# First weight loads issued in step with what has landed, low-rank factors behind the third unit, and the sums of squares at the third unit's first product

## The chip, the cores and the metric

The kernel runs on one core of a Trainium2 chip. The time is that of one execution on the device in microseconds (us). The engines are TensorE (PE, with its weight loads as PEld), VectorE (DVE), ScalarE (ACT), GpSimd (POOL) and SyncE (SP), which issues the transfers (DMAs) concerned here.

## The reference

Two blocks follow each other, all in float32. The first takes 256 tokens and 16 meta tokens of width 2048, normalises them and multiplies them by `w_in` (2048 x 8320). The change lies in this stretch:

```python
hn = _rmsnorm(h_res, norm_in_g[l])        # x * rsqrt(mean(x*x) + eps) * g
P = hn @ w_in[l]
Pr, Pc = P[..., :RW_COLS], P[..., RW_COLS:]
prev = jnp.pad(Pr[:, :-1], ((0, 0), (1, 0), (0, 0)))
Pr = Pr + (prev - Pr) * mu_shift[l]       # r, k, v, g_r, wl (64 cols), al (64 cols)
w_raw = -softplus(-(w0[l] + tanh(wl) @ w_lora_up[l])) - 0.5
a = sigmoid(a0[l] + al @ a_lora_up[l])
```

A recurrence over the tokens, a gated convolution and an output projection follow, then the second block: two attention layers of width 4096 with their projections, and a last norm.

## The kernel before

The norm is taken out of the product: PE multiplies the weights by x times the gain, and the product is scaled afterwards by the inverse root of the mean square (`rms_inv`). Weights and x are each split into a high and a low part (ACT makes the high part, `split_hi`, line 254; DVE the low part, `split_lo`, line 260), and PE makes three matmuls for each 128 x 128 tile (`product`, lines 275 to 277).

Weights come in units of 2048 x 128, each loaded in two halves of 512 KB (8 tiles of k; a half is 24 matmuls). A unit's raw halves lie in one of three slots (`rawa`), the splits in four buffers. The first unit is the low-rank one (`U_LORA`), then for each tile i of 128 channels come `row_unit(i, 0)` to `row_unit(i, 3)` for k, r, v and g, and behind these the convolution's units. For i = 0 the second unit is thus `row_unit(0, 0)`, the third `row_unit(0, 1)`, the fourth `row_unit(0, 2)`. Products go to two PSUM banks in turn; a bank is free when its product has been taken (`taken`).

The order on each engine is written by hand, one function for each engine:

- SP (`first_sync`) issues the gain, chunks 0 and 1 of x (544 KB each) with the halves of the first unit between them, chunks 2 and 3, both halves of `row_unit(0, 0)`, the parameters `prm` (56 KB), `lmu` (0.5 KB), `lora` (512 KB, the low-rank factors), and then one unit after another. `load_columns` issues both halves of a unit; it waits only for the low parts of the unit that had the slot before, which the second and third unit have none of.
- ACT (`first_act`) makes the high part of x by chunks, and of the first unit between them; then the split of the second unit's first half, the squares of x (line 402) between the splits that follow, the copy of the first unit's product, the root (`setup_root`, line 416), and the tanh of the low-rank product (line 712). Splits run `AHEAD` = 3 halves ahead of the product. A split of a unit's first half waits until both halves of the unit have landed (`landed`), except in the very first unit.
- DVE (`first_dve`) makes the low parts, folds the four chunks of squares into one (`setup_fold`, line 412), takes the reciprocal of the root (line 435) and from there on scales, shifts and evacuates products (lines 811 to 833), makes the decay's scan (lines 860 to 865) and the bonus product (line 881).
- PE (`first_pe`) runs the units in order. Smaller products are slipped in between tiles by a table of functions: `setup_sums` (line 430, four matmuls with ones, which sum the squares over the partitions) before tile 4 of the second half of `row_unit(0, 0)`; `gates(0)` (line 607) before tile 6 of the second half of `row_unit(0, 1)`; then `key_norm` (615) and `bonus` (622).

In `product` the wait for the low part of the half stands ahead of the loop over the tiles, and the slipped-in function is called inside that loop.

Of the kernel before, what the change touches and what calls it, by code (L numbers as in the profile page):

```python
# [29 lines left out]
P = 128  # L30
# [4 lines left out]
L = SEQ + META  # L35
CH = 1024
# [114 lines left out]
def wait(eng, sem, value):  # L151

    if isinstance(value, int) and value <= 0:
        return
    eng.wait_ge(sem, value)
# [7 lines left out]
def _build(nc, A, top):  # L163
# [3 lines left out]
    def sem(name):  # L167
        return top.enter_context(nc.semaphore(name))
# [6 lines left out]
    hi_ready = sem("hi_ready")  # L175
# [171 lines left out]
    x_in = [sem(f"x_in{c}") for c in range(4)]  # L347
# [17 lines left out]
    xh, xl = xhl[:, :, 0:L], xhl[:, :, 272:272 + L]  # L365
# [6 lines left out]
    def setup_loads(sp, c):  # L372
        if c == 0:
            sp.dma_start(gain[:], A["gain"]).then_inc(gain_in, 16)
        sp.dma_start(x0[:, chunks[c]], A["xt"][:, chunks[c]]).then_inc(x_in[c], 16)
# [49 lines left out]
    def setup_sums(pe):  # L425
        pe.wait_ge(pool_seq, 7)
        pe.wait_ge(sq_folded, XC - 1)
        n = KT // XC
        for k in range(n):
            mm = nc.tensor.matmul(psum[2][:, 0:L], ones[:], sq0[:, k], start=k == 0, stop=k == n - 1)  # L430
        mm.then_inc(rms_bcast, 1)
# [39 lines left out]
    FIRST = [0, META - 2, 0, META - 2]  # L471
    FIRST_CONV = [META - 2] * 4

    def first_phase():
# [6 lines left out]
        st = Stream(ph, "a", 3, 0, sem("begin_in"))  # L481
# [48 lines left out]
        w_in = A["w_in"].rearrange("(k p) n -> p k n", p=P)  # L530
        R_KINDS, C_KINDS = [1, 0, 2, 3], [5, 6, 4, 7]

        def row_unit(i, n):
            return At(U_IN + 4 * i + n)

        def conv_unit(i, n):
            return At(U_IN + 4 * CT + 4 * i + n)
# [9 lines left out]
        def first_sync(sp):  # L547
            low_rank = slice(4 * CH, 4 * CH + P)
            setup_loads(sp, 0)
            st.load_half(sp, 0, 0, w_in[:, 0:8, low_rank], P, st.begin_in)  # L550
            setup_loads(sp, 1)
            st.load_half(sp, 0, 1, w_in[:, 8:16, low_rank], P, st.raw_in[0])
            for c in range(2, XC):
                setup_loads(sp, c)

            def keep_aab(i):

                sp.wait_ge(aab_taken, 2 * (i + 1))
                dst = aab_d.rearrange("(t c) (p e) s u -> c p e s t u", c=TC, e=2)
                for c in range(TC):  # L560
                    w = slice(C * c, C * c + C)
                    for e in range(2):
                        sp.dma_start(dst[c, i, e], aab[w, NT * e:NT * e + NT, w]).then_inc(aab_out, 16)
            for i in range(CT):
                for n in range(4):
                    if n == 1 and i >= 2:
                        keep_aab(i - 2)
                    st.load_columns(sp, row_unit(i, n), w_in,
                                    slice(R_KINDS[n] * CH + i * P, R_KINDS[n] * CH + (i + 1) * P))
                    if (i, n) == (0, 0):  # L570
                        sp.dma_start(prm[:], A["prm"]).then_inc(prm_in, 16)
                        sp.dma_start(lmu[:], A["lmu"]).then_inc(lmu_in, 16)
                        sp.dma_start(lora, A["lora"]).then_inc(lmu_in, 16)
            for i in range(CT):
                for n in range(4):
                    if (i, n) == (0, 1):
                        keep_aab(CT - 2)
                    if (i, n) == (1, 1):
                        keep_aab(CT - 1)
                    if (i, n) == (1, 3):  # L580
                        sp.wait_ge(sys_zeroed, 2)
                        sp.wait_ge(aab_out, 32 * TC * CT)
                        sp.dma_start(sa[:, 0:C], aab_d[0:NA].rearrange("c h s t -> (c h) s t")).then_inc(sys_in, 16)
                        sp.dma_start(sa[0:HEADS, last_block, 0:H2], aab_d[NA, :, 0:H2, 0:H2]).then_inc(sys_in, 16)
                    col = RW_COLS + (C_KINDS[n] - 4) * CH + i * P
                    st.load_columns(sp, conv_unit(i, n), w_in, slice(col, col + P))
            sp.wait_ge(sys_out[1], 1)
            sp.dma_start(inv_d[NA], sx_last).then_inc(stored, 16)
            sp.wait_ge(sys_out[0], 1)
            sp.dma_start(inv_d[0:NA].rearrange("c h s t -> (c h) s t"), sx[:, 0:C]).then_inc(stored, 16)  # L590
            sp.wait_ge(stored, 32)

        def first_pe(pe):
            x_chunk = {4 * j: (lambda n: lambda: pe.wait_ge(x_low, n))(j + 1) for j in range(2)}
            x_rest = {4 * j: (lambda n: lambda: pe.wait_ge(x_low, n))(j + 3) for j in range(2)}
            st.unit(pe, At(U_LORA), L, xh, xl, (x_chunk, x_rest))

            def gates(i):
                def emit():
                    if i == 0:  # L600
                        pe.wait_ge(lmu_in, 32)
                        pe.wait_ge(lora_ready, 2)
                        pe.wait_ge(pool_seq, 10)
                    wait(pe, z_used, 2 * i)
                    for e in range(2):
                        r = slice(64 * e, 64 * e + 64)
                        mm = nc.tensor.matmul(psum[2 + e][:, 0:L], lora[r, i * P:(i + 1) * P], low[r, :], start=True,
                                              stop=True)
                    mm.then_inc(z_ready, 1)
                return emit  # L610

            def key_norm(i):
                def emit():
                    pe.wait_ge(ksq_ready, i + 1)
                    nc.tensor.matmul(psum[4][:, 0:L], blk[:], t["ksq"][:, 0:L], start=True,
                                     stop=True).then_inc(n2_ready, 1)
                return emit

            def bonus(i):
                def emit():  # L620
                    pe.wait_ge(rkm_ready, i + 1)
                    nc.tensor.matmul(psum[5][:, 0:L], blk[:], t["tk"][:, 0:L], start=True,
                                     stop=True).then_inc(bonus_ready, 1)
                return emit

            def within(i):

                def emit():
                    pe.wait_ge(kap_made, i + 1)
                    wait(pe, aab_taken, 2 * i)  # L630
                    for n in range(NT):
                        w = slice(TT * n, TT * n + TT)
                        for e in range(2):
                            r = slice(64 * e, 64 * e + 64)
                            mm = nc.tensor.matmul(psum[6 + e][0:TT, w], bk[r, i, 0, w], kr[r, i, 0, w], start=True,
                                                  stop=True)
                            if n == NT - 1:
                                mm.then_inc(aab_sum, 1)
                return emit
            for i in range(CT):  # L640
                st.unit(pe, row_unit(i, 0), L, xh, xl, ({4: gates(i)}, {2: within(i - 1)}) if i else ({}, {4: lambda: setup_sums(pe)}),
                        FIRST[0])
                st.unit(pe, row_unit(i, 1), L, xh, xl, ({}, {}) if i else ({}, {6: gates(i)}), FIRST[1])
                st.unit(pe, row_unit(i, 2), L, xh, xl, ({2: key_norm(i)}, {}), FIRST[2])
                st.unit(pe, row_unit(i, 3), L, xh, xl, ({2: bonus(i)}, {}), FIRST[3])
            for i in range(CT):
                for n in range(4):
                    st.unit(pe, conv_unit(i, n), L, xh, xl, ({}, {2: within(CT - 1)} if (i, n) == (0, 0) else {}),
                            FIRST_CONV[n])
# [122 lines left out]
        def first_dve(dve):  # L772
# [170 lines left out]
            for i in range(CT):  # L943
                def p(n):
                    return prm[:, i, n:n + 1]
                for n in range(4):
# [22 lines left out]
                    if n == 3:  # L969
                        wait(dve, yb_made, i)  # L970
                        scaled(q, pgc[:], META, taken[q.bank()])
        ph.close()
        return first_sync, first_pool, first_pe, first_act, first_dve
    first_sync, first_pool, first_pe, first_act, first_dve = first_phase()
    p01.close()
# [528 lines left out]
    st = Stream(ph, "b", 4, U_WOUT)  # L1504
# [872 lines left out]
```

## Time and profile before

| | us |
|---|---|
| median of 3 runs | 2449.84 |
| lowest, highest | 2449.75, 2450.86 |
| profiled execution, time | 2450.07 |
| profiled execution, span | 2448.3 |

| engine | busy us | share of span |
|---|---|---|
| PE | 2419.5 | 99% |
| PEld | 2155.8 | 88% |
| DVE | 1753.6 | 72% |
| ACT | 1222.5 | 50% |
| POOL | 309.1 | 13% |

The span goes from the first to the last instruction of the profiled execution; its time has some 1.8 us around that. Busy time of an engine is what its instructions cover, register, branch, semaphore and DMA-issuing instructions left out. What counts for the time is the engine that others wait for, and where it is idle. The timeline prints, behind an instruction, how long its engine was idle before it and who released it.

### The profile page before, as it was taken

The page shows a single profiled execution, that of the slowest core. Times are in us where ns is not written, and L with a number is a line of the kernel's source. Part 1 is how long each engine was busy: PE and PEld are TensorE (multiplying, and loading weights), DVE is VectorE, ACT ScalarE, POOL GpSimd, SP SyncE. Part 2 cuts the span into 40 slices and gives each one's busy share as a digit, 9 for nine tenths or more (in the row PEclk, how much of TensorE's full clock was granted, in tenths as well). Part 3 has the DMA queues.
Part 4 walks back from the last instruction along what each step waited for, and adds up shares of the span by engine and source line. Part 5 has one row for each costly group of instructions (what it writes and reads, how often), then busy time and mean ns, then how long its engine had stood idle before and what let it go on. Part 6 is the DMA issues. An engine that isn't in the chain of part 4 may idle for free.

```text
span 2448.3 us, 40487 instructions
## 1 busy us (share of the span) xinstructions
PE 2419.5 (99%) x16586; PEld 2155.8 (88%) x16586; DVE 1753.6 (72%) x2629; ACT 1222.5 (50%) x1811; POOL 309.1 (13%) x397
## 2 busy tenths in 40 slices
PE   7999999999999999999999999999999999999998
PEld 7999999888888888888888888888888888888887
DVE  8998797997767566766766668667576757676676
ACT  6555433665544445444545456545444444444445
POOL 1212114422100000000000002111010001000011
PEclk9999999999999999999999999999999999999999
DMA  8666773486567666666666665777667766767783
GB/s 220 175 160 175 199 187 86 112 220 197 168 189 197 189 181 179 192 177 194 180 197 188 177 177 170 196 189 186 197 174 193 196 187 186 189 188 181 194 195 107
DMA packets 758344, 443.31 MB, mean 181 GB/s; under 512 B 28784, under 2 KB 721136, under 8 KB 758160
## 3 DMA queue, kind: packets, MB, share of 16 engines
q1 hardware_dynamic: 752880, 430.16, 63.3%
q0 software_dynamic: 5280, 10.56, 3.3%
q8 instruction: 132, 2.16, 0.4%
q14 instruction: 52, 0.43, 0.1%
HBM read 437.35 MB, written 3.31 MB: 180 GB/s over the span
## 4 chain that ended last, share of the span: by engine, by line
PE 81%; DVE 3%; issue 1%; ACT 0%; DVEq 0%; ACTq 0%
PE bank L295 40%; PE bank L299 20%; PE bank L325 5%; PE bank L326 5%; PE bank L329 5%; PE bank L1863 1%; PE bank L1882 1%; PE bank L1870 1%; PE bank L1862 1%; PE bank L1883 1%; DVE splitb L260 0%; PE bank L275 0%; PE bank L277 0%; PE bank L276 0%; PE bank L1843 0%
## 5 line engine op out<-in xcount | busy, mean ns | idle before, releaser
L295 PE MATMUL bank<-xx,splitb 128*128 128x512 f32 x3328 | 1166.1, 396 | 1.4 <-DVE mix L2152 0.8
L260 DVE TENSOR_TENSOR splitb<-rawb,splitb 128x1024 fp32r<-128x1024 f32 x672 | 834.7, 1255 | 395.0 <-ACT splitb L254 388.5
L254 ACT ACTIVATE splitb<-rawb 128x1024 fp32r<-128x1024 f32 x672 | 701.3, 1055 | 503.0 <-PE bank L299 354.1
L299 PE MATMUL bank<-xx,splitb 128*128 128x256 f32 x3328 | 922.4, 277 | 0.0
L295 PEld LDWEIGHTS bank<-xx,splitb 128*128 128x128 f32 x3328 | 625.3, 188 | 130.7 <-DVE mix L2152 1.1
L299 PEld LDWEIGHTS bank<-xx,splitb 128*128 128x128 f32 x3328 | 625.5, 188 | 1.6
L295 PE MATMUL bank<-oo,splitb 128*128 128x512 f32 x1008 | 343.3, 389 | 0.0
L275 PE MATMUL bank<-xhl,splita 128*128 128x258 f32 (+1 forms) x1040 | 297.7, 286 | 12.5 <-DVE splita L260 11.2
L277 PE MATMUL bank<-xhl,splita 128*128 128x258 f32 (+1 forms) x1040 | 292.6, 281 | 0.0
L276 PE MATMUL bank<-xhl,splita 128*128 128x258 f32 (+1 forms) x1040 | 292.3, 281 | 0.0
L299 PE MATMUL bank<-oo,splitb 128*128 128x256 f32 x1008 | 278.2, 276 | 0.0
L295 PEld LDWEIGHTS bank<-oo,splitb 128*128 128x128 f32 x1008 | 189.2, 188 | 39.6
L275 PEld LDWEIGHTS bank<-xhl,splita 128*128 128x128 f32 x1040 | 196.1, 189 | 17.7 <-DVE splita L260 11.6
L254 ACT ACTIVATE splita<-rawa 128x1024 fp32r<-128x1024 f32 x130 | 136.9, 1057 | 134.4 <-PE bank L277 131.9
L325 PE MATMUL bank<-splitb,xx 128*128 128x512 f32 x512 | 199.5, 390 | 0.0
L326 PE MATMUL bank<-splitb,xx 128*128 128x512 f32 x512 | 198.8, 388 | 0.0
L276 PEld LDWEIGHTS bank<-xhl,splita 128*128 128x128 f32 x1040 | 196.3, 189 | 0.7
L277 PEld LDWEIGHTS bank<-xhl,splita 128*128 128x128 f32 x1040 | 196.1, 189 | 0.0
L260 DVE TENSOR_TENSOR splita<-rawa,splita 128x1024 fp32r<-128x1024 f32 x130 | 164.9, 1275 | 34.6 <-ACT splita L254 33.4
L299 PEld LDWEIGHTS bank<-oo,splitb 128*128 128x128 f32 x1008 | 189.2, 188 | 0.0
L2011 ACT ACTIVATE cross<-bank 128x256 f32<-128x256 f32 x192 | 72.9, 380 | 205.7 <-PE bank L299 205.7
L329 PE MATMUL bank<-splitb,xx 128*128 128x512 f32 x512 | 126.4, 388 | 0.0
(294 smaller groups left out, 2265.6 us busy)
## 6 DMA issues: line engine op xcount, KB each, us to landing
rawb<-in_a_w_in_dram SPq DMA_DIRECT2D x256, 512.0 KB, 4.9
rawa<-in_w_in_dram SPq DMA_DIRECT2D x130, 512.0 KB, 5.4
rawb<-in_kv_w_dram SPq DMA_DIRECT2D x128, 512.0 KB, 4.8
rawb<-in_b_w_in_dram SPq DMA_DIRECT2D x128, 512.0 KB, 5.4
rawb<-in_a_w_out_dram SPq DMA_DIRECT2D x64, 512.0 KB, 5.3
rawb<-in_b_w_out_dram SPq DMA_DIRECT2D x64, 512.0 KB, 5.3
rawb<-in_w_out_dram SPq DMA_DIRECT2D x32, 512.0 KB, 5.1
table<-in_rel_dram POOLq DMA_DIRECT2D x32, 128.0 KB, 4.5
```

The lines of the kernel that those rows point to most:

```text
L254: nc.scalar.activation(self.parts(at, h)[0], self.raw_half(at, h), ACT.Copy).then_inc(hi_ready, 1)
L260: nc.vector.tensor_tensor(lo, self.raw_half(at, h), hi.bitcast(F32), ALU.subtract).then_inc(lo_ready, 1)
L275: nc.tensor.matmul(out, hi[:, w], rhs_hi(k), start=start and k == 0, stop=False)
L276: nc.tensor.matmul(out, hi[:, w], rhs_lo(k), start=False, stop=False)
L277: last = nc.tensor.matmul(out, lo[:, w], rhs_hi(k), start=False, stop=stop and k == 7)
L295: nc.tensor.matmul(out, hi[:, w], both(k).rearrange("p a t -> p (a t)"), start=start and k == 0, stop=False)
L299: last = nc.tensor.matmul(out[:, 0:SEQ], lo[:, w], both(k)[:, 0], start=False, stop=stop and k == 7)
L325: nc.tensor.matmul(out, xx[:, kt, 0, tokens], hi[:, w], start=kt == 0, stop=False)
L326: last = nc.tensor.matmul(out, xx[:, kt, 1, tokens], hi[:, w], start=False, stop=kt == KT - 1)
L329: last = nc.tensor.matmul(out, xx[:, kt, 0, tokens], lo[:, w], start=False, stop=False)
L1862: nc.tensor.matmul(SC[:, 0:P], qT[:, 0:P], kT[:, 0:P], start=True, stop=True)
L2011: a(cross[:, at.bank()], GB[at.bank()][:, SEQ:], ACT.Copy).then_inc(crossed, 1)
```

## The change

In SP's order, the first half of `row_unit(0, 0)` is issued when chunk 2 of x has landed, and the second half when chunk 3 has. The parameters and the first half of `row_unit(0, 1)` are issued when three halves of weights have had their high part made (`hi_ready` at 3: both halves of the first unit and the first of `row_unit(0, 0)`). The second half of `row_unit(0, 1)` is issued when `row_unit(0, 0)` has landed whole, then `lmu` and `lora`, which thereby stand behind `row_unit(0, 1)` instead of ahead of it. The fourth unit is issued when `row_unit(0, 1)` has landed whole. On PE, `setup_sums` moves from tile 4 of the second half of `row_unit(0, 0)` to tile 0 of the first half of `row_unit(0, 1)`, behind that half's wait for its low part. Nothing is computed otherwise.

```diff
--- before.py
+++ after.py
@@ -565,12 +565,23 @@
                 for n in range(4):
                     if n == 1 and i >= 2:
                         keep_aab(i - 2)
-                    st.load_columns(sp, row_unit(i, n), w_in,
-                                    slice(R_KINDS[n] * CH + i * P, R_KINDS[n] * CH + (i + 1) * P))
+                    cols = slice(R_KINDS[n] * CH + i * P, R_KINDS[n] * CH + (i + 1) * P)
                     if (i, n) == (0, 0):
+                        sp.wait_ge(x_in[2], 16)
+                        st.load_half(sp, 1, 0, w_in[:, 0:8, cols], P, st.raw_in[1])
+                        sp.wait_ge(x_in[3], 16)
+                        st.load_half(sp, 1, 1, w_in[:, 8:16, cols], P, st.raw_in[1])
+                    elif (i, n) == (0, 1):
+                        sp.wait_ge(hi_ready, 3)
                         sp.dma_start(prm[:], A["prm"]).then_inc(prm_in, 16)
+                        st.load_half(sp, 2, 0, w_in[:, 0:8, cols], P, st.raw_in[2])
+                        sp.wait_ge(st.raw_in[1], 32)
+                        st.load_half(sp, 2, 1, w_in[:, 8:16, cols], P, st.raw_in[2])
                         sp.dma_start(lmu[:], A["lmu"]).then_inc(lmu_in, 16)
                         sp.dma_start(lora, A["lora"]).then_inc(lmu_in, 16)
+                        sp.wait_ge(st.raw_in[2], 32)
+                    else:
+                        st.load_columns(sp, row_unit(i, n), w_in, cols)
             for i in range(CT):
                 for n in range(4):
                     if (i, n) == (0, 1):
@@ -638,9 +649,8 @@
                                 mm.then_inc(aab_sum, 1)
                 return emit
             for i in range(CT):
-                st.unit(pe, row_unit(i, 0), L, xh, xl, ({4: gates(i)}, {2: within(i - 1)}) if i else ({}, {4: lambda: setup_sums(pe)}),
-                        FIRST[0])
-                st.unit(pe, row_unit(i, 1), L, xh, xl, ({}, {}) if i else ({}, {6: gates(i)}), FIRST[1])
+                st.unit(pe, row_unit(i, 0), L, xh, xl, ({4: gates(i)}, {2: within(i - 1)}) if i else ({}, {}), FIRST[0])
+                st.unit(pe, row_unit(i, 1), L, xh, xl, ({}, {}) if i else ({0: lambda: setup_sums(pe)}, {6: gates(i)}), FIRST[1])
                 st.unit(pe, row_unit(i, 2), L, xh, xl, ({2: key_norm(i)}, {}), FIRST[2])
                 st.unit(pe, row_unit(i, 3), L, xh, xl, ({2: bonus(i)}, {}), FIRST[3])
             for i in range(CT):
```

## Rows read from the trace of the kernel before

**Rows 1.** The page's first part: engine, busy us, share of the span, instructions.

```profile
PE 2419.5 (99%) x16586; PEld 2155.8 (88%) x16586; DVE 1753.6 (72%) x2629; ACT 1222.5 (50%) x1811; POOL 309.1 (13%) x397
```

**Rows 2.** Windows: start:end, length, busy us (instructions) by engine, clock, DMA share, GB/s.

```profile
30.00:52.00 22.00, 21.25 (x165) 19.69 (x164) 20.06 (x32) 12.80 (x19) 5.22 (x5) 1.00 0.49 134
...
52.00:370.00 318.00, 318.00 (x2688) 311.94 (x2686) 278.33 (x419) 154.86 (x191) 62.12 (x64) 1.00 0.68 180
```

**Rows 3.** Timeline of PE: start us, us, engine, line, op, tiles, [idle before, releaser].

```profile
9.86 0.59 PE L275 MATMUL bank<-xhl,splita 128*128 128x272 f32 x1 [9.86 <-DVE splita L260]
...
19.45 0.39 PE L275 MATMUL bank<-xhl,splita 128*128 128x272 f32 x1 [1.37 <-DVE splita L260]
...
25.35 2.07 PE L430 MATMUL bank<-bk,ones 128*128 128x272 f32 x8 [0.93 <-DVE bk L412]
...
33.70 0.73 PE L607 MATMUL bank<-area 64*128 64x272 f32 x4
...
42.82 0.73 PE L622 MATMUL bank<-area,blk 128*128 128x272 f32 x2 [0.38 <-DVE area L881]
...
48.83 0.40 PE L275 MATMUL bank<-xhl,splita 128*128 128x272 f32 x1 [0.37 <-DVE area L811]
```

**Rows 4.** Timeline of ACT, columns as in rows 3.

```profile
17.08 1.06 ACT L254 ACTIVATE splita<-rawa 128x1024 fp32r<-128x1024 f32 x1 [1.67 <-DMA rawa<-in_w_in_dram]
...
23.00 1.05 ACT L254 ACTIVATE splita<-rawa 128x1024 fp32r<-128x1024 f32 x1
...
27.46 0.49 ACT L416 ACTIVATE rms_inv<-bank,eps 128x272 f32<-128x272 f32 x1 [2.19 <-PE bank L430]
...
28.91 1.28 ACT L712 ACT_TABLE_LOAD   x1
...
31.69 0.43 ACT L712 ACTIVATE area<-area 64x272 f32<-64x272 f32 x1 [1.50 <-DVE area L833]
...
34.59 0.52 ACT L717 ACTIVATE area<-area,prm_sb 128x272 f32<-128x272 f32 x1 [0.92 <-DVE area L824]
```

**Rows 5.** Timeline of DVE, columns as in rows 3.

```profile
18.18 1.22 DVE L260 TENSOR_TENSOR splita<-rawa,splita 128x1024 fp32r<-128x1024 f32 x1 [1.91 <-ACT splita L254]
...
22.52 2.68 DVE L412 TENSOR_TENSOR bk<-bk 128x1088 f32<-128x1088 f32 x2
...
27.98 1.85 DVE L435 RECIPROCAL rms_inv<-rms_inv 128x272 f32<-128x272 f32 x1 [0.43 <-ACT rms_inv L416]
...
39.68 1.23 DVE L260 TENSOR_TENSOR splita<-rawa,splita 128x1024 fp32r<-128x1024 f32 x1 [1.11 <-ACT splita L254]
```

**Rows 6.** DMA issues from 3.29, 5.92, 6.39, 6.87, 14.82 us: KB, us to landing.

```profile
kr<-in_xt_dram SPq DMA_DIRECT2D x1, 544.0 KB, 8.7
...
kr<-in_xt_dram SPq DMA_DIRECT2D x1, 544.0 KB, 7.5
...
rawa<-in_w_in_dram SPq DMA_DIRECT2D x1, 512.0 KB, 8.8
...
rawa<-in_w_in_dram SPq DMA_DIRECT2D x1, 512.0 KB, 10.2
...
rawa<-in_w_in_dram SPq DMA_DIRECT2D x1, 512.0 KB, 7.3
```

**Rows 7.** DMA issues into an empty queue, from 35.66, 36.07, 43.93, 44.34 us.

```profile
rawa<-in_w_in_dram SPq DMA_DIRECT2D x1, 512.0 KB, 4.1
...
rawa<-in_w_in_dram SPq DMA_DIRECT2D x1, 512.0 KB, 5.4
...
rawa<-in_w_in_dram SPq DMA_DIRECT2D x1, 512.0 KB, 4.3
...
rawa<-in_w_in_dram SPq DMA_DIRECT2D x1, 512.0 KB, 6.1
```

**Rows 8.** Line groups of PE, 9.8 to 14 us, then 14 to 18 us.

```profile
L276 PE MATMUL bank<-xhl,splita 128*128 128x272 f32 x6 | 2.5, 411 | 0.0
...
L276 PE MATMUL bank<-xhl,splita 128*128 128x272 f32 x10 | 2.9, 285 | 0.0
```


## Prediction

> **What bounds the kernel now.** Units of weights are called u0 (low rank), u1, u2, u3 in the order of their loads, their halves a and b; the chunks of x are x0 to x3. I read the page's engine line first: TensorE (PE) is busy 2419.5 us of 2448.3 [rows 1]. Then the table of stretches: from 52 to 370 us PE has no idle time, and in the first 52 us it has what a change of the first loads can reach [rows 2]. Third, PE's timeline. It shows an idle start of 9.86 us; 1.37 us before unit 1's first half; 0.93 us before the sums of squares; 0.38 and 0.37 us at 42.82 and 48.83 us [rows 3]. Behind the start that is 3.05 us in all, and the start itself is set by u0 and the first two chunks of x, whose issue is untouched. So removing every later stall gives 3.05 us, 0.12%.
>
> ScalarE's (ACT's) timeline says which wait ends last: the split of u1 begins at 17.08 us, released by its DMA. It needs both halves of u1, though only half a is split there. u2's split at 23.00 us follows ACT's own work without idle time [rows 4]. The VectorE (DVE) timeline then gives the second chain: folds of the squares to 25.2 us, root, reciprocal from 27.98 us, and from there DVE and ACT hand to each other up to 39.68 and beyond [rows 5]. PE's waits at 42.82 and 48.83 us are for DVE, at the end of this chain [rows 3]. **The root of the mean square is therefore on the path that sets the end**, with no slack left at 42.82 us.
>
> Last, the DMA issues. The queue delivered in order and without a hole: x2 is landed at 3.29 + 8.7 = 11.99 us, x3 at 5.92 + 7.5 = 13.42, u1b at 6.87 + 10.2 = 17.07, u2b at 14.82 + 7.3 = 22.12 [rows 6]. Into an empty queue a half of 512 KB takes 4.1 to 4.3 us; the second of the pair lands 36.07 + 5.4 - 35.66 = 5.81 us or 44.34 + 6.1 - 43.93 = 6.51 us after the first one's issue [rows 7].
>
> **Part 1, waits ahead of u1's halves.** Half a is issued at 12.05 us instead of 6.39, half b at 13.5 instead of 6.87. Nothing else of SP's is due before them. Half a lands after 4.1 to 4.3 us, at 16.2 to 16.4; half b no earlier than 13.5 + 4.1 = 17.6, and by the pairs 1.7 us behind half a (39.76 to 41.47), so 17.9; by the slower pair 2.2 us behind (48.23 to 50.44), 18.6. I take 17.9, as half b's own latency points lower. ACT's split of u1a moves from 17.08 to 17.95 us: **+0.9**. Do x2 and x3 land sooner for it? They stood ahead of u1 in a queue that delivers in order; nothing to gain that I can see. PE begins u1 at 20.3 instead of 19.45 us.
>
> **Part 2, u2 behind the third split.** SP now waits until u1a is split: ACT start to DVE start was 17.08 to 18.18, 1.10 us [rows 4, 5], so 19.05 us. Queued behind this wait are prm, u2 and u3, lmu and lora. prm costs 0.4 us of issue and 56 KB. u2a is issued at 19.5 us, u2b at 19.9 instead of 14.82 (its wait on u1 is long over). u2b lands 5.8 to 6.5 us after 19.5: 25.3 to 26.0 instead of 22.12. Two rows lie at either end, so I take the middle, 25.65.
> ACT is ready for u2a at 23.00 + 0.9 = 23.9 us, so it now waits some 1.7 us for data. Split 25.65, plus 1.10 to DVE, plus 1.27 to PE (18.18 to 19.45 [rows 3, 5]): u2a's low part is ready at 28.0 us.
>
> **Part 3, the sums of squares behind the wait of u2's product.** DVE's folds end near 25.2 + 0.9 = 26.1 us. PE, from 20.3 us: it did one and a half halves in 25.35 - 0.93 - 19.45 = 4.97 us [rows 3], at most 3.3 per half, so u1 is done by 26.9. Left in place, the sums would start at 26.1; at the new place they start when the low part of u2a is ready, 28.0. They take 25.35 to 27.46 = 2.11 us to the root [rows 3, 4]: root at 30.1 instead of 27.46, **+2.65**. The 0.93 us stall is gone, and about 1.1 to 1.5 us before the sums stand in its place.
>
> **Part 4, lora and lmu behind u2.** Issued at 20.4 to 20.8 us, queued behind u2b: 27 us. DVE needs lmu only behind the reciprocal (27.98 + 1.85, plus 2.65: 32.5 us), PE needs lora later. Cover of over 5 us, cost nothing; uncovered, it would cost what exceeds that.
>
> **Part 5, u3 behind the landing of u2.** Issue 25.7 us, landed both halves 31.5 to 32.2 [rows 7]; 2.7 us after u2b u3a would have queued anyway, so this wait is felt less. ACT can then split u3a (1.07 us), load its table (1.28 us): ready at 33.9 to 34.6. The tanh was at 31.69 [rows 4] and moves with the root to 34.3. So +0 to 0.3 there, and PE's gate products (33.70 [rows 3]) come to 35.2 or so: PE waits a little. None of this sets the end, because ACT's square of k (34.59 [rows 4]), on DVE's chain, moves to 37.2 and the tanh of the gates follows it. u4 and u5 are issued behind u3 and lie over 4 us ahead of their splits.
>
> **Sum.** The chain root, reciprocal, low-rank shift, k, scan, exponentials, split of u4, PE's waits at 42.82 and 48.83 us contains no DMA that is now late and no PE step that ends last, so it moves as a whole: PE is 2.65 us later at 45.5 us. Behind it PE is never idle up to 370 us [rows 2], and the other engines move with it. The profiled execution took 2450.07 us (span 2448.3), 0.23 above the median of the three; 2450.07 + 2.65 - 0.23 = **2452.5 us**. That is +0.11%, within the 0.2% (4.9 us) that a measurement of this kernel can tell from no change.
>
> The bounds of this case: if half b of u1 lands at 17.6 and u2 after 5.8, the shift is 2.65 - 0.3 - 0.35 = 2.0; at 18.6 and 6.5, 2.65 + 0.7 + 0.35 = 3.7: 2451.8 to 2453.5.
>
> **A rule that speaks otherwise.** The rows give 4.1 to 4.3 us for a lone half. The Trainium skill (DMA: Bandwidth & Descriptors, section Anatomy of one DMA) gives a fixed 2.0 us plus bytes at 436 GB/s, measured on GpSimd's path: an estimate of 3.2 us here, 4.4 for the pair. By it the reloads would nearly catch up, which is rival A's outcome; the rows here, on SP's queue, are longer.
>
> **Rivals.**
> A. **The loads stay hidden.** If the waits shorten each load's own time (fewer packets in flight), by 1.4 us on the last half of each pair, u1 lands as before and u2b by 23.8 us. Then u2a is ready at 23.8 + 2.4 = 26.2, PE finishes u1 at 25.6 to 26.1, and the root is at 28.3: +0.2 to +0.9 us, 2450.0 to 2450.8. For it: u1b took 10.2 us from its issue [rows 6], so the queue was full. Against: the rows from an empty queue already hold that advantage.
> B. **The change gains.** If the reloads are hidden and the 0.93 us stall counted on PE's path, PE ends 0.5 to 1 us earlier: 2449. Against: PE then waits at 42.82 us, since DVE's chain does not move forward.
> C. **The clock falls, ending on the slower side.** PE's idle time ahead of u1 grows from 1.37 to 2.2 us, a length that no stretch between PE's first matmul and the end shows. Matmuls of the same shape took 411 ns at PE's start and 285 ns once it had worked for about 4 us [rows 8]: the two levels, 1.2 and 2.4 GHz, although the printed granted clock doesn't resolve it. If the level falls there, u1a's 24 matmuls cost 24 x 0.126 = 3.0 us; 1.1 to 1.3 are covered by the wait for u2, the rest delays the root: 2454.2 to 2454.5.
> D. **Round trips add up.** Three load pairs in series (u1, u2, u3), each at the 6.5 us end, and lora's 512 KB between u2 and u3: u1b 18.6, u2b 26.8, u3b 33.4 to 34.7 us. The latter decides from 32.3 us on, as ACT's split and table load then hold the tanh: +4 to +5 us, 2454 to 2455; with C, over +4.9, slower by more than 0.2%.
> E. **The waits do nothing** (all met on arrival): 2449.8 to 2450.1. Against: x2 and x3 land 5.6 and 6.6 us after u1's present issues (11.99 - 6.39, 13.42 - 6.87) [rows 6].
>
> **Chances.** Forecast 0.62; A with E 0.14; B 0.05; C 0.07; D 0.12, of it 0.03 beyond 4.9 us. Range from A's lower end to D's beginning, 2450.0 to 2454.3, leaves out B, a part of C and D. Faster by over 0.2%: 0.01, since only 3.05 us are to be had. Slower by over 0.2%: 0.03. Within: 0.96.
>
> **What would show it.** Landing of u1b at 17.6 to 18.6 and u2b at 25 to 26.5 us; ACT idle about 1.7 us, released by DMA, before the split of u2a; the sums right before u2's first product at about 28 us; the root at 30; PE idle over 1 us at about 45 us for DVE L881; then PE without a gap to 370 us. The prediction is wrong if x3 or u1 lands earlier than now, if u2's split doesn't wait for data, or if the root moves by 2.65 us and the end doesn't.

## The result: slower by 3.7 us, and where it arises

The changed kernel took 2453.75 us (median of 20 runs, 2451.54 to 2455.7) against 2450.01 us for the kernel before (20 runs, 2448.31 to 2451.61). The ratio is 1.0015, with a 95% interval of 1.0009 to 1.0021: 2.2 to 5.1 us slower. The forecast was 2452.5 us, in a range of 2450.0 to 2454.3.

| | before | after |
|---|---|---|
| median, us | 2450.01 | 2453.75 |
| profiled execution, time | 2450.07 | 2454.09 |
| its span | 2448.3 | 2452.4 |
| PE busy, us | 2419.5 | 2420.1 |
| last chunk of x landed | 13.4 | 13.2 |
| u1a split begins (ACT) | 17.08 | 18.50 |
| u2a split begins (ACT) | 23.00 | 26.11 |
| sums of squares begin (PE) | 25.35 | 28.52 |
| root (ACT) | 27.46 | 30.63 |
| last early wait of PE ends | 48.83 | 52.00 |

The units are named as in the prediction (u0 to u3, halves a and b). ACT's timeline of the changed kernel answers to [rows 4]; the columns are start us, us, engine, line, operation, tiles, and the idle time before with its releaser:

```profile
18.50 1.06 ACT L254 ACTIVATE splita<-rawa 128x1024 fp32r<-128x1024 f32 x1 [3.11 <-DMA rawa<-in_w_in_dram]
...
26.11 1.06 ACT L254 ACTIVATE splita<-rawa 128x1024 fp32r<-128x1024 f32 x1 [1.59 <-DMA rawa<-in_w_in_dram]
...
30.63 0.49 ACT L416 ACTIVATE rms_inv<-bank,eps 128x272 f32<-128x272 f32 x1 [2.24 <-PE bank L430]
32.01 1.06 ACT L254 ACTIVATE splita<-rawa 128x1024 fp32r<-128x1024 f32 x1 [0.89 <-DMA rawa<-in_w_in_dram]
33.09 1.28 ACT L722 ACT_TABLE_LOAD   x1
34.87 0.43 ACT L722 ACTIVATE area<-area 64x272 f32<-64x272 f32 x1 [0.49 <-DVE area L843]
...
37.76 0.52 ACT L727 ACTIVATE area<-area,prm_sb 128x272 f32<-128x272 f32 x1 [0.93 <-DVE area L834]
```

Where ACT had one wait for weights before, of 1.67 us, it now has three: 3.11 us for u1, 1.59 for u2, 0.89 for u3. The root is at 30.63 instead of 27.46 us, 3.17 later, and so is everything behind it: the square of k (L727) at 37.76 instead of 34.59. PE's timeline answers to [rows 3]:

```profile
20.87 0.39 PE L275 MATMUL bank<-xhl,splita 128*128 128x272 f32 x1 [2.79 <-DVE splita L260]
...
28.52 1.84 PE L430 MATMUL bank<-bk,ones 128*128 128x272 f32 x7 [1.22 <-issue]
...
45.99 0.72 PE L633 MATMUL bank<-area,blk 128*128 128x272 f32 x2 [0.54 <-DVE area L891]
...
52.00 0.40 PE L275 MATMUL bank<-xhl,splita 128*128 128x272 f32 x1 [0.38 <-DVE area L821]
...
389.57 0.39 PE L275 MATMUL bank<-xhl,splita 128*128 128x258 f32 x1 [0.87 <-DVE cv L978]
...
2443.61 0.88 PE L1954 MATMUL bank<-sc,ones 128*128 128x128 f32 x4 [0.65 <-DVE sc L2329]
```

PE's stall before u1 has grown from 1.37 to 2.79 us, that before the sums from 0.93 to 1.22, and the wait for DVE's bonus product ends at 45.99 instead of 42.82 us. From 52.00 on PE is 3.17 us late, and it is 3.17 us late at 389.57 (386.40 before) too. At 2443.61 it is 4.01 us late. The 0.84 us between can't be put down to the change, because executions scatter by more than that behind the start: two executions of one kernel (e6 and e12 below) pass their last early wait at 46.87 and 46.82 us, 1.96 and 2.01 ahead of before, and this last PE row at 2436.57 and 2438.65, 3.03 and 0.95 ahead of before's 2439.60.

The windows of the start answer to [rows 2]; busy us (instructions) of PE, PEld, DVE, ACT and POOL, then clock, share of the DMA engines and GB/s:

```profile
10.00:20.00 10.00, 7.75 (x48) 7.29 (x48) 6.31 (x14) 6.60 (x13) 0.00 (x0) 1.00 0.58 186
20.00:30.00 10.00, 7.91 (x55) 7.31 (x56) 8.19 (x8) 6.80 (x8) 0.00 (x0) 1.00 0.84 239
...
55.00:373.00 318.00, 318.00 (x2687) 311.93 (x2687) 278.35 (x419) 154.87 (x191) 62.02 (x63) 1.00 0.68 180
```

Before, the same columns read, from 10 to 20 us:

```profile
10.00:20.00 10.00, 8.63 (x52) 8.26 (x53) 7.20 (x14) 8.04 (x14) 0.00 (x0) 1.00 1.13 328
```

The DMA engines moved 328 GB/s then and 186 now: the waits leave the queue empty from 18.5 us, where u1b has landed, to 19.6, and nearly so from 12 to 14 us (88 GB/s, before 309). The transfers themselves (issues from 11.97, 13.27 and 19.96 us; KB and us to landing) answer to [rows 6] and [rows 7]:

```profile
rawa<-in_w_in_dram SPq DMA_DIRECT2D x1, 512.0 KB, 4.1
...
rawa<-in_w_in_dram SPq DMA_DIRECT2D x1, 512.0 KB, 5.2
...
rawa<-in_w_in_dram SPq DMA_DIRECT2D x1, 512.0 KB, 4.4
```

u1a landed 4.1 us after its issue, u1b 5.2 us, so at 18.5 us; u2a 4.4 us, and ACT was released by u2b at 26.1.

### The profile page after: what moved, and what is told of

The parts are those of the page before. It is cut to its first block, busy times and chain, and to the rows that moved or that the text cites. A ratio compares the mean times of both kernels' runs of the same rounds, so it can differ in the third digit from the quotient of the medians.

```text
span 2452.4 us, 40488 instructions
## 1 busy us (share of the span) xinstructions
PE 2420.1 (99%) x16586; PEld 2155.5 (88%) x16586; DVE 1756.0 (72%) x2629; ACT 1222.7 (50%) x1811; POOL 307.7 (13%) x397
## 4 chain that ended last, share of the span: by engine, by line
PE 82%; DVE 2%; issue 1%; ACT 0%; DVEq 0%; ACTq 0%
PE bank L295 40%; PE bank L299 20%; PE bank L325 5%; PE bank L326 5%; PE bank L329 5%; PE bank L1873 1%; PE bank L1892 1%; PE bank L1880 1%; PE bank L1872 1%; PE bank L1893 1%; DVE splitb L260 0%; PE bank L275 0%; PE bank L277 0%; PE bank L276 0%; PE bank L1286 0%
```

## How the experiments are read

The loss is some 3 us of 2450, and the medians of 11 runs carry an interval of about +-2 us; e5, e7, e8, e9 and e10 have one execution each, whose time decides nothing. Positions in a trace are finer, but there is one trace for each kernel, and the landing of x shifts the whole start by up to 0.5 us between executions. So two distances are used. **D1** is when ACT begins to split u1a; it moves with the loads. **D2** is the time from there to the end of PE's last early wait. In the kernel before they are 17.08 and 48.83 - 17.08 = 31.75 us; in the changed kernel 18.50 and 33.50: +1.42 and +1.75, together 3.17. In the kernel with only `lora` moved D2 is 31.76, with D1 at 16.61, so D2 doesn't depend on the phase of x. D1 and the last mark do. The last column takes the phase out: it counts the last mark from where ACT begins on x2 (12.00 us in the kernel before, 11.97 in the changed one, 11.53 to 12.02 in all), so from 36.83 us in the kernel before.

| kernel | D1 | D2 | last mark | against 48.83 | the same, from x2 |
|---|---|---|---|---|---|
| before | 17.08 | 31.75 | 48.83 |  |  |
| after | 18.50 | 33.50 | 52.00 | +3.17 | +3.20 |
| e1, sums moved alone | 16.68 | 32.84 | 49.52 | +0.69 | +1.11 |
| e2, loads alone | 18.23 | 32.08 | 50.31 | +1.48 | +1.72 |
| e3, after, u1 at once | 16.80 | 33.93 | 50.73 | +1.90 | +1.97 |
| e4, after, u2 and u3 at once | 18.11 | 33.37 | 51.48 | +2.65 | +3.12 |
| e5, before, lora behind u2 | 16.61 | 31.76 | 48.37 | -0.46 | -0.04 |
| e6, before, u1a waited for alone | 15.14 | 31.73 | 46.87 | -1.96 | -1.78 |
| e7, before, one square first | 16.69 | 30.88 | 47.57 | -1.26 | -0.86 |
| e8, e2 without u3's wait | 18.45 | 31.78 | 50.23 | +1.40 | +1.47 |
| e9, e4 with PE kept busy | 18.78 | 32.84 | 51.62 | +2.79 | +3.20 |
| e10, after, u1a waited for alone | 16.09 | 33.39 | 49.48 | +0.65 | +0.63 |
| e11, e6 with squares on POOL | 15.13 | 34.61 | 49.74 | +0.91 | +1.09 |
| e12, e6 again | 15.08 | 31.74 | 46.82 | -2.01 | -1.77 |

The theory is that of the prediction: the root of the mean square heads a chain that PE waits for at 42.82 and 48.83 us, and three edits push it. The rival is that one part makes all of the loss, the others being hidden.

## The sums alone, and the loads alone

In e1 only the place of the sums differs from before, in e2 only the loads. The edit of e1, abridged to the tables of slipped-in functions that `row_unit(i, 0)` and `row_unit(i, 1)` get for i = 0:

```diff
-  row_unit(i, 0) ... ({}, {4: lambda: setup_sums(pe)})
-  row_unit(i, 1) ... ({}, {6: gates(i)})
+  row_unit(i, 0) ... ({}, {})
+  row_unit(i, 1) ... ({0: lambda: setup_sums(pe)}, {6: gates(i)})
```

> The kernel before, with only the sums of squares moved to the first product of u2. My theory (the root of the mean square is on the path, and the sums now stand behind u2a's low part): that part is made at 25.12 to 26.34 us, so the sums start at 26.4 instead of 25.35 us, the root at 28.5 instead of 27.46, and every later mark of PE (42.82, 48.83 us) comes 1.0 to 1.1 us later; PE stalls some 0.4 to 0.7 us ahead of the sums instead of 0.93. Time +1 us. Rival (the place of the sums is free, all of the loss is the loads'): root within 0.2 us of 27.46 and marks unmoved.

Measured: D2 +1.09 us. The sums began at 26.04 us, 9.36 us behind u1a's split, where before it was 8.27:

```profile
26.04 1.84 PE L430 MATMUL bank<-bk,ones 128*128 128x272 f32 x7 [0.54 <-issue]
```

DVE makes u2a's low part only behind its folds, so the sums now wait for one instruction more, which ended at 25.93:

```profile
24.71 1.22 DVE L260 TENSOR_TENSOR splita<-rawa,splita 128x1024 fp32r<-128x1024 f32 x1
```

The stall before the sums shrank from 0.93 to 0.54 us, and yet the root came later: a shorter stall of PE at this place is not a gain, as PE does u1's last four tiles first and has the root wait for it and for u2a. The median was 2451.67 us, ratio 1.0005 (0.9996 to 1.0014), which alone decides nothing. The marks do: the rival, a free place, is out.

> The changed order of the loads alone; the sums stay inside the second half of u1. My theory: u1's split at 18.5 us shifts the folds by 1.4 us, the sums start at 26.7, the root is at 28.9, marks +1.4 us; u2's later landing (26.1 us) costs nothing, as PE is busy with the sums and the rest of u1 until 30.2 us. So of the 3.17 us of the changed kernel the two parts give 1.05 + 1.4 alone, and 0.7 us arises only where both are together. Rival (the late u2 costs by itself): marks +2 us or more, with PE idle before u2's first product.

Measured: D1 +1.15 (+1.39 counted from x2), D2 +0.33, the last mark +1.48; ratio 1.0006 (0.9997 to 1.0015). The root was at 28.60 us, +1.14, all of it D1. The expectation missed that the mark came 0.34 us later than the root. ACT's timeline shows what took over:

```profile
28.60 0.49 ACT L416 ACTIVATE rms_inv<-bank,eps 128x272 f32<-128x272 f32 x1 [0.45 <-PE bank L430]
31.84 1.07 ACT L254 ACTIVATE splita<-rawa 128x1024 fp32r<-128x1024 f32 x1 [2.75 <-DMA rawa<-in_w_in_dram]
32.93 1.28 ACT L723 ACT_TABLE_LOAD   x1
34.22 0.43 ACT L723 ACTIVATE area<-area 64x272 f32<-64x272 f32 x1
```

The root was made in time, but then ACT waited 2.75 us for u3, and the table load for the tanh stands behind u3a's split. The tanh starts at 34.22 us with no idle time before it, 5.62 us behind the root; before, it was 31.69 - 27.46 = 4.23, and released by DVE [rows 4].

To see whether that is u3's wait, e8 takes the wait out of e2.

```diff
-                        sp.wait_ge(st.raw_in[2], 32)
```

> The kernel of the run with the loads alone (sums at their old place), without the wait for u2's landing ahead of u3. There the root was at 28.60 us (+1.14) but PE's last early wait at 50.31 (+1.48); u3 landed at 31.8, ACT split its half a at 31.84 and loaded the table of the tanh behind it. Theory (u3's landing takes over by 0.34 us): u3 lands near 29.5, and the last mark comes as much later than 48.83 us as the root than 27.46, so +1.1 to +1.2. Rival (the 0.34 us come from the gate products or from PE's order): root and mark stay apart by 0.3 us or more.

Measured: D2 31.78 us, before's own, with root and mark at +1.36 and +1.40. So ACT's split of u3a, released by the DMA at 30.94 instead of 31.84 us, was in time; the 0.33 us were u3's wait. The root came 0.2 us later than expected, with D1 (18.45). In the changed kernel the same wait costs nothing: u3a is split at 32.01, and the tanh at 34.87 is released by DVE after 0.49 us of idle time.

## Each wait taken out of the changed kernel

```diff
# e3
-                        sp.wait_ge(x_in[2], 16)
...
-                        sp.wait_ge(x_in[3], 16)
# e4
-                        sp.wait_ge(hi_ready, 3)
...
-                        sp.wait_ge(st.raw_in[1], 32)
...
-                        sp.wait_ge(st.raw_in[2], 32)
```

> The changed kernel without the two waits ahead of u1's halves; all else as changed. My theory: u1 lands at 17.1 us again, u1a is split by 18.2, and from there u2b takes the 6.5 us that it took in the changed kernel: 24.7 us, the sums start at 27.1, the root at 29.2, marks +1.7 to +1.8 us instead of +3.17. Rival (u2's wait alone sets the root, u1's throttling is hidden, for example because x2 and x3 land sooner with it): marks stay at +3.2 us, x3 lands later than 13.24 us.

Measured: D1 back at 16.80, D2 33.93, the last mark at +1.90; ratio 1.0009 (1.0 to 1.0018). The rival falls: u1's waits are not hidden. D2 is 0.43 us longer than in the changed kernel, as ACT was released by u2b 8.02 us behind u1a's split there (24.82 - 16.80) and 7.61 in the changed kernel (26.11 - 18.50). x3 landed at 13.3 us there and at 13.2 in the changed kernel, so holding u1 back brought x 0.1 us at most.

> The changed kernel without the three waits around u2 and u3, those ahead of u1's halves kept. My theory: u1 as in the changed kernel (split at 18.5 us), u2b lands at about 22.1, well before ACT comes to it at 24.4 us; its low part is ready at 27.8, root at 29.9, marks +2.4 to +2.5 us. Rival (the loss comes from u2's wait alone): marks back to +1.05 us or less.

Measured: +2.65 us at the last mark (+3.12 from x2), and not the +1.05 of the rival; ratio 1.0016 (1.0007 to 1.0025). But D2 was 33.37, where 31.75 + 1.09 = 32.84 was due. u2a's low part was made at 27.36 us, and the sums began at 28.07. PE's windows say why:

```profile
18.00:20.40 2.40, 0.00 (x0) 0.00 (x0) 1.20 (x1) 2.29 (x3) 0.00 (x0) 1.00 1.22 289
20.40:24.00 3.60, 3.52 (x16) 3.52 (x17) 2.82 (x4) 3.60 (x4) 0.00 (x0) 0.55 1.14 327
24.00:28.00 4.00, 4.00 (x34) 4.00 (x33) 3.90 (x5) 2.30 (x4) 0.00 (x0) 0.98 1.20 290
```

From 20.4 to 24 us the granted clock was 0.55 of full speed, between the levels of 2.4 and 1.2 GHz and mostly at the lower one, after PE had been idle for 2.84 us. From 20.8 to 24.1 alone it was at the lower one:

```profile
20.80:24.10 3.30, 3.30 (x17) 3.30 (x16) 2.90 (x3) 3.30 (x5) 0.00 (x0) 0.50 1.12 325
```
Line 276's matmuls (the columns are out<-in, shapes, count, then busy us and mean ns) took 416 ns from 20 to 24 us, and 286 ns in the changed kernel:

```profile
L276 PE MATMUL bank<-xhl,splita 128*128 128x272 f32 x5 | 2.1, 416 | 0.0
```

```profile
L276 PE MATMUL bank<-xhl,splita 128*128 128x272 f32 x8 | 2.3, 286 | 0.0
```

In e9, 18 matmuls whose results nobody reads stand between u0 and u1.

```diff
             st.unit(pe, At(U_LORA), L, xh, xl, (x_chunk, x_rest))
+            for _ in range(18):
+                nc.tensor.matmul(psum[7][:, 0:L], xhl[:, 0, 0:P], xhl[:, 0, 0:L], start=True, stop=True)
```

> The kernel of the run with u2 at once, with 18 more matmuls on PE between u0 and u1, whose results nobody reads, to fill the 2.8 us in which PE stood idle there. In that run the granted clock was 0.55 of full speed from 20.4 to 24 us, u1 took 7.5 us of PE instead of 6.44, and the sums started at 28.07 us although u2a's low part was there at 27.36. Theory (the clock fell because PE was idle): granted clock 1.00 throughout, u1 done 6.4 to 6.5 us after its start at about 20.5, sums at 27.4, root at 29.5 and PE's marks some 0.6 us earlier than in that run. Rival (the clock fell for another reason, or the slow matmuls were contention with loads): u1 takes over 7 us again. The fill itself costs nothing, as it ends before u1's low part is there.

Measured: the granted clock is 1.00 in both windows, u1 takes 6.44 us again, and D2 is 32.84, to the hundredth that of e1. u1 landed later in this execution (D1 18.78; u1b took 5.9 us from its issue, in e4 5.3), so the marks themselves are not earlier; the distance is. That the clock fell because of the idle time fits this pair; but PE was idle for 2.79 us in the changed kernel, 2.76 in e2 and 2.81 in e8 and the clock stayed at full speed in their profiles. Those three differ from e4 in one thing more: their matmuls had been at the short spacing since 12.53 to 12.89 us, e4's since 13.85 only. What decides between them isn't shown.

```profile
17.50:20.40 2.90, 2.46 (x20) 2.23 (x18) 0.52 (x1) 1.62 (x2) 0.00 (x0) 1.00 1.15 294
20.40:24.00 3.60, 2.84 (x23) 2.84 (x24) 2.83 (x3) 3.60 (x5) 0.00 (x0) 1.00 1.03 309
```

So the changed kernel's 3.17 us are made up of 1.42 (u1 split later), 1.09 (the sums behind u2a) and the rest, 0.66 (u2 landing later than ACT comes to it), which exists only because the sums stand behind u2a: in e2 and e8, with the sums at their old place, u2's late landing doesn't move the root (10.37 us behind u1a's split in both, before 10.38).

## Order of lora, and what would have helped

e5 issues `lmu` and `lora` behind u2 in the kernel before.

> The kernel before with lmu and lora issued behind u2 instead of ahead of it, nothing else. Theory (u2 is not waited for in the kernel before, and lora has over 5 us to spare): u2b lands near 20.9 instead of 22.14 us and lora near 22.1, ACT comes to u2a at 23.0 as before, root 27.46 give or take 0.4 us (the phase of x's landing), PE's waits as before. Rival (the order of lora is worth something): root or last mark more than 0.4 us off what x3's landing explains.

Measured: D2 31.76, the root 10.38 us behind u1a's split as before (26.99 - 16.61; 27.46 - 17.08), time 2450.43 us. This part is free, and brings nothing.

ACT waits for both halves of u1 although it splits only half a. In e6 half a of u1 has its own semaphore; all loads are issued as before.

```diff
+    next_in = sem("next_in")
...
+                        st.load_half(sp, 1, 0, w_in[:, 0:8, cols], P, next_in)
+                        st.load_half(sp, 1, 1, w_in[:, 8:16, cols], P, st.raw_in[1])
...
-            apart = 16 if self.begin_in is not None and n % self.slots == 0 else 0
+            apart = 16 if self.begin_in is not None and n % self.slots in (0, 1) else 0
...
-            if self.begin_in is not None and (at.u, h) == (self.first, 0):
-                act.wait_ge(self.begin_in, 16)
+            if self.begin_in is not None and h == 0 and at.u - self.first in (0, 1):
+                act.wait_ge(self.begin_in if at.u == self.first else next_in, 16)
...
```

> The kernel before with one thing changed: u1a has a semaphore of its own, so that ACT splits it when half a has landed (15.2 us) and not when both have (17.1). Theory (what bounds the start of the chain is ACT's wait for u1b, 1.67 us): split at 15.4 us, PE goes from u0 to u1 with next to no idle time (1.37 us before), folds end at 23.6, sums at 23.7, root at 25.8, marks 1.5 to 1.7 us earlier than before. Time -1.6 us. Rival (the early stalls are hidden behind DVE's chain or the loads): marks within 0.3 us of before.

Measured: D1 15.14, D2 31.73, the last mark 1.96 us earlier (1.78 from x2). The stall of 1.37 us before u1 is gone; that before the sums stays:

```profile
23.39 1.84 PE L431 MATMUL bank<-bk,ones 128*128 128x272 f32 x7 [0.93 <-DVE bk L413]
...
46.87 0.40 PE L275 MATMUL bank<-xhl,splita 128*128 128x272 f32 x1 [0.38 <-DVE area L816]
```

The median was 2448.86 us against 2450.29, ratio 0.9993 (0.9984 to 1.0002). e12 is the same kernel again.

> The kernel with the half wait once more, since its first comparison gave 0.9993 with an interval that touches 1, and its marks say -1.7 to -2.0 us. Theory: the same marks within 0.4 us, and a median 1.5 to 2 us below before, 0.9992 to 0.9994. Rival (the early gain is given back later in the kernel): marks as before, but median within 0.5 us of before.

Measured: last mark 46.82, median 2449.15 against 2450.60 us, ratio 0.9994 (0.9985 to 1.0003). Both medians are 1.4 us lower, near the 1.8 us of the marks, but each interval still holds 1: the marks show the gain at the start, the time doesn't yet prove it at the end.

e10 puts the same semaphore into the changed kernel; u2b's issue then waits for u1b alone.

> The changed kernel with a semaphore of its own for u1a, so that ACT splits it when half a has landed (16.08 us in the changed kernel) and not when both have (18.5). Theory (issuing by halves costs what it does because the halves are still consumed together): u1a is split at 16.1 us, SP goes on at 17.2 instead of 19.58, u2b lands 6.5 us later, at 23.7, its low part is ready at 26.1, the root is at 28.2, marks +0.7 to +0.8 us against before instead of +3.17. Rival (the latency of the transfers alone is the loss): marks at +2 us or more.

Measured: split at 16.09, u2 at 23.58, root at 28.11, last mark +0.65 instead of +3.17 us; time 2452.62. So the marks come 2.5 us earlier than in the changed kernel: the issues of u2 hang on u1a's split, and this no longer on u1b. But that doesn't make the whole-unit wait the cause of 2.5 of the 3.2 us, since the same semaphore gains 1.8 to 2.0 us in the kernel before (e6). Against e6, which also takes u1 by halves, e10 is 2.61 us late (49.48 and 46.87), 2.41 from x2: the change costs most of its 3.2 us there too.

e7 lets ACT square x0 while it waits for u1, in the kernel before.

```diff
+            setup_square(act, 0)
             hi(row_unit(0, 0), 0)
-            setup_square(act, 0)
             setup_square(act, 1)
```

> The kernel before with the square of x0 ahead of the split of u1a on ACT, in the 1.67 us for which ACT waits for u1 (15.41 to 17.08 us). Theory (the folds, so ACT's squares, set the sums): ACT has 1.0 us less to do behind the split, folds end at about 24.2 instead of 25.2 us, the stall of 0.93 us before the sums is gone, root at 26.5, marks 0.9 to 1.0 us earlier. Rival (PE's own order sets the chain): root within 0.2 us of 27.46.

Measured: D2 30.88, 0.87 us shorter; the sums' stall shrank to 0.31 us, the root came at 26.20. ACT's squares and DVE's folds set the sums here, not PE's order, and PE has 0.31 us left to give.

Last, e11 gives the squares of x0 and x1 and their fold to POOL, in e6, and takes them from ACT and DVE. POOL's part of the edit:

```diff
+        for c in range(2):
+            pool.wait_ge(x_in[c], 16)
+            g.tensor_tensor(sq0[:, chunks[c]], x0[:, chunks[c]], x0[:, chunks[c]], ALU.mult).then_inc(pool_sq, 1)
+        pool.wait_ge(pool_sq, 2)
+        g.tensor_tensor(sq0[:, chunks[0]], sq0[:, chunks[0]], sq0[:, chunks[1]], ALU.add).then_inc(sq_folded, 1)
```

> The kernel with the half wait, and with the squares of x0 and x1 and their fold made by POOL, idle from 5.4 us on, instead of ACT and DVE. Theory (the chain ahead of the sums is ACT's squares and DVE's folds): DVE's last fold ends at about 22 instead of 23.3 us, PE goes into the sums without idle time at 22.1, the root is at 24.3 instead of 25.50, marks 1.0 to 1.2 us earlier than with the half wait alone, some 3 us earlier than before. Time about -3 us. Rival (POOL is too slow for it, or slows DVE beside it): POOL's three instructions end behind 19 us, or DVE's instructions of the same shapes take longer than 1.22 and 1.29 us, and the gain is under 0.5 us.

Measured: the rival, and more than it. The root was at 28.37 us, 2.9 later than in e6, the last mark +0.91, ratio 1.0007 (0.9998 to 1.0016). POOL ended in time, at 14.7 us:

```profile
5.49 2.00 POOL L402 TENSOR_TENSOR bk<-kr 128x1088 f32<-128x1088 f32 x1
8.74 3.27 POOL L402 TENSOR_TENSOR bk<-kr 128x1088 f32<-128x1088 f32 x1 [1.26 <-DMA kr<-in_xt_dram]
12.09 2.58 POOL L404 TENSOR_TENSOR bk<-bk 128x1088 f32<-128x1088 f32 x1
```

But DVE's low parts of x, made beside it, took 5.71 us for four where e6 took 1.73 (start us, us; first e11, then e6):

```profile
6.07 2.96 DVE L448 SCALAR_TENSOR_TENSOR xhl<-kr,gain,xhl 128x272 fp32r<-128x272 f32 x4 [2.60 <-ACT xhl L429]
8.94 1.22 DVE L260 TENSOR_TENSOR splita<-rawa,splita 128x1024 fp32r<-128x1024 f32 x1
10.08 5.71 DVE L448 SCALAR_TENSOR_TENSOR xhl<-kr,gain,xhl 128x272 fp32r<-128x272 f32 x4
```

```profile
6.24 1.74 DVE L443 SCALAR_TENSOR_TENSOR xhl<-kr,gain,xhl 128x272 fp32r<-128x272 f32 x4 [2.78 <-ACT xhl L424]
8.40 1.23 DVE L260 TENSOR_TENSOR splita<-rawa,splita 128x1024 fp32r<-128x1024 f32 x1 [0.42 <-ACT splita L254]
9.54 1.73 DVE L443 SCALAR_TENSOR_TENSOR xhl<-kr,gain,xhl 128x272 fp32r<-128x272 f32 x4
```

Taken one by one, three of these eight took 1.72, 2.23 and 2.73 us (from 6.07, 10.08 and 12.24 us) instead of 0.49, and ended at 7.79, 12.31 and 14.97, each 0.30 us behind the end of one of POOL's (7.49, 12.01, 14.67). It goes the other way too: DVE's subtraction of 128 x 1024 at 8.94 ran beside POOL's second square and took its usual 1.22 us, and that square took 3.27 instead of 2.00 us. So these rows look as if one of the two engines stood still until the other's instruction had ended, though POOL's spans are rough. The Trainium skill (SBUF — State Buffer, section Who interferes with whom) says that a DVE instruction with two SBUF inputs contends with a GpSimd instruction that reads SBUF; both kinds of instruction are that here, and the trace agrees.

PE then waited for the late low parts in the middle of u0 (2.54 us before 15.85, 1.11 before 18.73), so it ended u1 at 26.33 us and went into the sums without idle time, while DVE's folds had ended at 25.10: here it is PE that sets the sums.

## Why the prediction was right, and which term was off

**What bounds the kernel: right.** The root heads the chain; its 3.17 us reappear to the hundredth at 45.99, 52.00 and 389.57 us. The forecast put the delay into one idle time of over 1 us at about 45 us; it was 0.54 us there, as PE had lost most of it before: 1.42 us more before u1, 0.29 more before the sums, 0.35 before the gate products and 0.22 at 44.48.

**Part 1, u1: right mechanism, under-sized.** Half b was taken to land at 17.9 us, with 18.6 as the other end; it landed at 18.5, so +1.42 instead of +0.9. The step that failed is the choice between the pairs of [rows 7]: u1b came 2.4 us behind u1a, not 1.7. It took 5.2 us from its issue, like the second of a pair (5.4 and 6.1 in [rows 7]), although it was issued 1.3 us behind the first. "As half b's own latency points lower" was the wrong reason: 4.1 us is what a load takes alone. x3 landed at 13.2 us instead of 13.4. Taken by the letter that is a sign of being wrong that the prediction named; but 0.2 us is less than executions scatter, and counted from x2 it is 0.1 at most, so in substance it was right that x gains nothing.

**Part 2, u2: right.** From u1a's split to u2b's landing 7.7 us were forecast (17.95 to 25.65), 7.6 measured (18.50 to 26.1); ACT's wait was put at 1.7 us and was 1.59.

**Part 3, the sums: right.** 28.0 us forecast, 28.52 measured, and part 1's error of 0.55 covers the difference. The sums' own 2.11 us held. That they cost time at the new place even without the loads is e1's 1.09 us.

**Part 4, lora: right** (e5). **Part 5, u3: right in the changed kernel**, where it is hidden by 0.49 us; in e2, without the later sums, it is the next wait, worth 0.33.

**The sum** gave +2.65 us; +3.17 us is what the start measures, within the stated bounds of 2.0 to 3.7. The remaining 0.6 of the median's +3.74 lies inside its interval and isn't attributed to anything; with it the median, 2453.75, is 0.25 us above the upper of these bounds (2453.5), and inside the wider range only because that reached to the rivals C and D.

**The rivals.** A (loads stay hidden) fell: lone halves took 4.1 and 4.4 us, not 3.2. The rule of the Trainium skill that the prediction set against it (DMA: Bandwidth & Descriptors, Anatomy of one DMA) is about a us short on this queue. B fell with it. C (the clock) did not occur in the changed kernel's profile but did in e4's, where the idle time before u1 was 2.84 us and u1 became 1.15 us longer (7.59 instead of 6.44), of which 0.53 us delayed the chain (33.37 - 32.84). C's price of 1.7 us beyond the cover was too high, as the clock was back soon after 24 us (0.98 in the window from 24 to 28) and a slow matmul began 0.23 us behind the last one instead of 0.12, so cost 0.10 and not 0.126. Whether C struck in other executions of the changed kernel is open: the mean granted clock of a whole execution was 0.997 in 5 of e4's 11, its profile among them, in 4 of the changed kernel's 20 and in none of the 78 of the kernel before that ran beside the experiments (otherwise 0.998 or 0.999), and 3.4 us at half the clock lower this mean by 0.0007; but e6, where PE hardly idles, has one at 0.997 too. D fell: only u1 was at the slow end. E fell: three waits were felt.

## To carry to other kernels

Holding a load back until earlier ones have landed hardly speeds those up when the queue already delivers in order (x3: 0.1 us at most); it adds a load's full time from an empty queue, here 4 to 5 us each time. A consumer that works in the smaller pieces is worth its edit by itself (e6, 1.8 us), but did not make the held-back loads free: between e6 and e10 the change still costs 2.4 us. Moving a small product "to where PE doesn't wait" is decided by who waits for its result: here the stall got shorter and the kernel longer. Measure such edits by distances between marks in the trace, as medians cannot resolve 1 us in 2450.

## What the runs showed of the hardware

- Gaps of 2.76 to 2.84 us on PE were followed by the lower clock in one profile of four (0.50 from 20.8 to 24.1 us in e4); gaps of up to 1.62 us (e3) never were, nor was the 2.54 us in e11. So slow matmuls (416 against 286 ns) behind a gap of this length are possible, not certain, and the profiles don't show what decides.
- Two-input DVE instructions that began beside a two-input POOL instruction on the same memory ended 0.30 us behind it and took 1.72 to 2.73 us instead of 0.49 (e11); once DVE's took its usual time and POOL's 3.27 instead of 2.00 us. It made the idle engine's help cost 2.9 us.
- A half issued 1.3 us behind another into an otherwise empty queue took 5.2 us, 1.1 more than the first.
- Two executions of one kernel that are level at 48 us can be 2 us apart at the end (e6 and e12: 0.05 and 2.08 us).
